# One scatter per pair of expert items on all 128 rows, and the last 2 MB of weights by output column, in a hybrid decoder layer on one core

## Chip, cores and metric

One core of a Trainium2 chip runs the whole program in one launch. The metric is the device time of that core in microseconds (us); lower is better. The engines are TensorE (PE; its weight loads are PEld), VectorE (DVE), ScalarE (ACT), GpSimd (POOL) and SyncE (SP), which here issues nearly all transfers. All data is float32.

## What is computed

A decoder layer on 256 tokens of width 1024: sparse attention and an RWKV-7 mixer behind one input projection, an output projection, cross-attention into 256 memory tokens, and last a mixture of 32 experts, of which each token takes 4. The change lies in the experts, whose reference is, in short:

```python
logits = xt @ router_w + router_b
top_v, top_i = lax.top_k(logits, 4)
gate = jax.nn.softmax(top_v)
# for each expert e, with the tokens tok that chose it and their gates wr:
hb = x[tok] @ mlp1_w[e] + mlp1_b[e]                 # 1024 -> 2048
hg = jnp.minimum(hb[..., ::2], 7.0)
hl = jnp.clip(hb[..., 1::2], -7.0, 7.0)
yb = (hg * sigmoid(1.702 * hg) * (hl + 1)) @ mlp2_w[e] + mlp2_b[e]   # 1024 -> 1024
y[tok] += yb * wr[:, None]
return h + y
```

## The kernel before, in words

An *item* is one expert with up to 64 of its tokens (slots); two items make a pair (`par` 0 is the even, 1 the odd one), so that 128 slots are filled by one gather. In this execution there are 32 items. The weights of one item, 24576 columns of 128 rows (12.58 MB), go through one buffer, `ring`, in six pieces of 2 MB: pieces 0 to 3 hold `mlp1_w`, 4 and 5 hold `mlp2_w`. A piece of the next item is loaded into the place of the same piece as soon as TensorE has used it: SP waits on `piece_used` and issues the load, TensorE waits on `piece_in_c` in `landed` before it reads. Items 6 to 27 are loaded two pieces at a time ("coarse"); for items 10 to 20 1 MB each was loaded earlier into buffers that were free, and POOL copies it into `ring`.

On TensorE an item is written out by hand, in this order: `hidden_bias` (4 products), `hidden` half 0 (pieces 0 and 1, 16 products of 64 slots by 512 columns, two at a time on the two halves of the array's columns), `turn_gates` (two transposes of the gates into PSUM bank 7, which DVE copies to `selgT[par]`), `hidden` half 1 (pieces 2 and 3), `turn_act` of half 0 (two transposes of the activations), `scatter` of the item before (4 products: 64 slots' sums in `yb`, times `selgT`, into four PSUM banks that hold 256 tokens by 1024 columns until the end), `turn_act` of half 1, for an odd item `gather` of the next pair (16 products), and `second` (pieces 4 and 5, 16 products into bank 7). DVE does the clamps and products between them, ACT the sigmoid and the copies of the turned activations and of bank 7 to `yb`. The sums of `yb` hold output columns 0 to 511 in rows 0 to 63 and columns 512 to 1023 in rows 64 to 127 (`o2` is 0 or 1), so each product of `scatter` contracts over 64 rows, and the two of one token tile stand on different rows of the array.

The last item differs: the scatter of the item before stands after piece 0, `turn_act` of half 0 after piece 2, and the end of `mlp2_w` comes in smaller loads (`late_in_0` to `late_in_2`). After it `yb` is copied in two halves of 256 columns, a scatter of 8 products of 256 columns follows, DVE and ACT copy the four PSUM banks out (512 columns each), and SP and ACT issue four stores of 256 KB. The residual `h` is added into the four banks by products with the identity ahead of the last pair (`for bank in range(4)`).

A float32 matmul leaves two records in the trace, so 4 products show as x8.

## Time and profile before

| | |
|---|---|
| runs of the kernel before | 1250.0 us median of 3 (1249.6 to 1250.23) |
| the profiled execution's own time | 1248.68 us |
| its span | 1246.8 us |
| granted TensorE clock, mean | 0.998 |
| weights of 32 items | 32 x 12.58 = 402.7 MB |

The span begins with the first instruction and ends with the last; the execution's own time is 1.9 us longer. The experts' products start at 351.6 us of the span and go on to its end. In a row of the profile, "busy" is the time in which an engine had an instruction at work, "xN" is how many there were, and "idle" with an arrow is what ended a wait. An answer on one DMA issue gives the time from the start of the issuing instruction to the landing of its last byte.

### The profile page before, as it was taken

The numbers are of one execution on the slowest core, as the hardware profiler recorded it, in microseconds if no ns is written. First come the engines' busy times: TensorE is split into PE (matmuls) and PEld (weight loads), VectorE is DVE, ScalarE is ACT, GpSimd is POOL, SyncE is SP. The second block draws the span as 40 slices with busy tenths as digits, with TensorE's granted clock in tenths as the row PEclk, the third lists the DMA queues.
The fourth block names the chain that finished last, engine by engine and source line by source line (L and its number), as shares of the span: only waits on it lengthen the run. The fifth ranks groups of instructions, "written<-read, shape, count | busy, mean of one in ns | idle before, by whom it ended". The sixth has DMA issues, their size and how long they took to land.

```text
span 1246.8 us, 19008 instructions
## 1 busy us (share of the span) xinstructions
PE 1211.5 (97%) x7700; PEld 612.0 (49%) x7700; DVE 373.3 (30%) x855; ACT 191.1 (15%) x435; POOL 76.8 (6%) x118
## 2 busy tenths in 40 slices
PE   9999999999999999999899999999999898989998
PEld 8888778888844343324334343443333232333332
DVE  4457784314064121212122122221212121212111
ACT  2332357214110000000000000000000000000001
POOL 7210012010100000000000001000000000000000
PEclk9999999999999999999999999999999999999999
DMA  7333212394789999999999999999999999999997
GB/s 267 135 137 132 103 37 71 141 427 175 304 340 425 427 428 429 437 429 432 430 433 432 433 430 432 429 432 431 435 423 430 432 433 433 429 429 429 429 427 308
DMA packets 27982, 442.46 MB, mean 355 GB/s; under 512 B 3104, under 2 KB 3232, under 8 KB 5664
## 3 DMA queue, kind: packets, MB, share of 16 engines
q1 hardware_dynamic: 27072, 440.23, 83.9%
q10 hardware_dynamic: 864, 1.57, 0.4%
q8 instruction: 34, 0.56, 0.2%
q14 instruction: 12, 0.10, 0.0%
HBM read 440.75 MB, written 1.05 MB: 354 GB/s over the span
## 4 chain that ended last, share of the span: by engine, by line
PE 75%; DMA 21%; DVE 2%; ACT 1%; issue 1%; SPq 0%; ACTq 0%; POOL 0%; DVEq 0%; POOLq 0%
PE ps L1010 29%; DMA sb_ring<-in_mlp_w 21%; PE ps L1052 11%; PE ps L332 8%; PE ps L986 3%; PE ps L976 3%; PE ps L832 2%; PE ps L783 2%; PE ps L692 2%; PE ps L998 2%; PE ps L1038 1%; PE ps L345 1%; PE ps L567 1%; PE ps L433 1%; PE ps L416 1%
## 5 line engine op out<-in xcount | busy, mean ns | idle before, releaser
L1010 PE MATMUL ps<-sb_ring,sb_xv 128*64 128x512 f32 x2048 | 455.7, 597 | 23.7 <-DMA sb_ring<-in_mlp_w 23.5
L1010 PEld LDWEIGHTS ps<-sb_ring,sb_xv 128*64 128x64 f32 x2048 | 142.1, 137 | 312.0 <-issue 279.6
L1052 PE MATMUL ps<-sb_ring,sb_xv 128*64 128x512 f32 x1024 | 227.0, 595 | 0.3
L1656 DVE TENSOR_SCALAR sb_early<-ps 128x256 f32<-128x256 f32 x64 | 27.2, 425 | 625.1 <-PE ps L1010 619.8
L1052 PEld LDWEIGHTS ps<-sb_ring,sb_xv 128*64 128x64 f32 x1024 | 72.7, 137 | 131.1 <-issue 129.0
L1697 ACT ACTIVATE sb_early<-sb_early 128x256 f32<-128x256 f32 (+2 forms) x69 | 28.2, 408 | 507.1 <-DVE sb_early L1656 500.7
L1697 ACT ACTIVATE sb_early<-ps 128x512 f32<-128x512 f32 (+2 forms) x39 | 21.1, 543 | 274.8 <-PE ps L1052 265.0
L986 PE MATMUL ps<-sb_early 64*128 64x512 f32 x248 | 61.6, 615 | 0.0
L332 PE MATMUL ps<-sb_hnT,sb_wsl 128*128 128x256 f32 x256 | 56.1, 379 | 0.0
L976 PE MATMUL ps<-sb_early,sb_hnT 128*128 128x128 f32 x480 | 56.0, 275 | 0.0
L976 PEld LDWEIGHTS ps<-sb_early,sb_hnT 128*128 128x128 f32 x480 | 54.8, 192 | 0.0
L332 PEld LDWEIGHTS ps<-sb_hnT,sb_wsl 128*128 128x128 f32 x256 | 48.7, 190 | 7.0 <-issue 0.5
L1626 DVE TENSOR_TENSOR sb_xv<-ps,sb_xv 128x512 f32<-128x512 f32 x32 | 22.1, 692 | 54.3 <-PE ps L976 54.0
L1163 DVE SCALAR_TENSOR_TENSOR sb_early<-sb_early 128x256 f32<-128x256 f32 x64 | 37.5, 587 | 2.2
L1038 PEld LDWEIGHTS ps<-sb_ident,sb_xv 128*128 128x128 f32 x128 | 12.9, 141 | 50.9 <-issue 26.0
L998 PE MATMUL ps<-sb_early,sb_hot 32*64 32x512 f32 x256 | 35.9, 613 | 0.0
L692 PE MATMUL ps<-sb_wsl,sb_ox 128*128 128x256 f32 x128 | 31.6, 391 | 0.0
L986 PEld LDWEIGHTS ps<-sb_early 64*128 64x128 f32 x248 | 21.4, 186 | 20.4 <-issue 20.4
L1697 ACT ACTIVATE sb_xv<-ps 128x256 f32<-128x256 f32 x64 | 24.0, 375 | 47.5 <-PE ps L1038 47.5
L1038 PE MATMUL ps<-sb_ident,sb_xv 128*128 128x128 f32 x128 | 28.0, 301 | 0.5 <-DVE sb_xv L1663 0.3
L832 PE MATMUL ps<-sb_hnT,sb_wsl 128*128 128x256 f32 x128 | 28.3, 381 | 0.0
L332 PE MATMUL ps<-sb_ox,sb_wsl 128*128 128x256 f32 x128 | 28.1, 379 | 0.0
(370 smaller groups left out, 1015.5 us busy)
## 6 DMA issues: line engine op xcount, KB each, us to landing
sb_ring<-in_mlp_w SPq DMA_DIRECT2D x55, 4096.0 KB, 19.1
sb_ring<-in_mlp_w SPq DMA_DIRECT2D x54, 2048.0 KB, 17.5
sb_ring<-in_mlp_w SPq DMA_DIRECT2D x11, 3072.0 KB, 15.6
sb_wsl<-in_w_front SPq DMA_DIRECT2D x31, 1024.0 KB, 4.8
sb_ring<-in_mlp_w SPq DMA_DIRECT2D x10, 1024.0 KB, 7.5
sb_wsl<-in_mlp_w SPq DMA_DIRECT2D x3, 1024.0 KB, 8.9
sb_spare<-in_mlp_w SPq DMA_DIRECT2D x2, 1024.0 KB, 9.3
sb_ring<-in_mlp_w SPq DMA_DIRECT2D x4, 512.0 KB, 13.0
```

The costliest lines, as they stand in the source:

```text
L332: mm = pe.matmul(t[:, g * T:(g + 1) * T], w[:, k, g * P:(g + 1) * P], act[:, k, :], start=k == 0, stop=k == KD - 1)
L692: return pe.matmul(t[:, 0:T], memT[:, k, tt * P:(tt + 1) * P], wjob(J_XV[j])[:, k, :], start=k == 0, stop=k == KD - 1)
L832: mm = pe.matmul(t[:, g * T:(g + 1) * T], w[:, k, g * P:(g + 1) * P], hnT[:, k, :], start=k == 0, stop=k == KD - 1)
L976: mm = pe.matmul(psum[:, 4 + k // 4, k % 4 * PAIR:(k % 4 + 1) * PAIR], h[:, tt, k * P:(k + 1) * P], sel[:, tt, :], start=tt == 0, stop=tt ...
L986: mm = pe.matmul(psum[:, 2 * tt + o2, :], selgT[par][r, tt, :], yb[r, :], start=False, stop=False, skip_group_check=True)
L998: return pe.matmul(psum[64 * half:64 * half + 64, 4 + n, :], hot[r, :], bias1[r, :], start=not last, stop=last)
L1010: mm = pe.matmul(psum[64 * half:64 * half + 64, 4 + n, :], xgT[:, k, SLOTS * par:SLOTS * par + SLOTS], ring[:, at + 512 * half:at + 512 * ...
L1038: mm = pe.transpose(psum[:, 6, m * P:(m + 1) * P], actv[:, m * P:(m + 1) * P], ident[:, :])
L1052: mm = pe.matmul(psum[64 * o2:64 * o2 + 64, 7, :], actT[:, 2 * n + m, 64 * q:64 * q + 64], ring[:, at + 512 * o2:at + 512 * o2 + 512], sta ...
L1163: return dve.scalar_tensor_tensor(out=o, in0=x, scalar=s, in1=y, op0=op0, op1=op1)
L1656: dve.tensor_scalar(gl, psum[:, 4 + n, 0:256], 7.0, None, ALU.min).then_inc(sem("glu"), 1)
L1697: return act.activation(o, x, func, **kw)
```

## The change

Sums. `yb` becomes two buffers. An even item's sums go as before to rows 0 to 63 (left columns) and 64 to 127 (right columns) of bank 7; an odd item's go the other way round (`rows(par, o2)`). So `yb[0]` gets the left columns of both items of a pair, one on rows 0 to 63 and one on 64 to 127, and `yb[1]` the right columns. `selgT[o2]` is filled to match, in two copies of 64 rows instead of one of 128. ACT copies bank 7 in two instructions of 64 rows.

Scatter. One scatter per pair of 4 products that contract over all 128 rows. It stands in the even item, after pieces 0 and 1, ahead of `turn_gates`; an odd item has none.

Turns. `turn_act` of half 0 stands in the middle of `hidden` half 1, `turn_act` of half 1 in the middle of piece 4. The gather of the next pair stands between pieces 4 and 5.

Last 2 MB. `mlp2_w`'s second half (piece 5) is laid out by output column: first the columns 0 to 255 of both sides, then 256 to 511. In the loop the product over it reads two blocks of 256 columns, 2048 apart. In the last item the sums of the first 256 columns stay in bank 7 and those of the others go to bank 4; the first are scattered and stored (`last_scatter(0)`) ahead of the wait for `late_in_2`, the others after the last product (`last_scatter(1)`). The residual is added to the left banks by DVE at the end, and only banks 1 and 3 get identity products. There are eight stores of 128 KB instead of four of 256 KB.

```diff
-            def scatter(par):
+            def scatter(cols=slice(0, 512)):
                 for tt in range(TT):
                     for o2 in range(2):
-                        r = slice(64 * o2, 64 * o2 + 64)
-                        mm = pe.matmul(psum[:, 2 * tt + o2, :], selgT[par][r, tt, :], yb[r, :],
+                        mm = pe.matmul(psum[:, 2 * tt + o2, cols], selgT[o2][:, tt, :], yb[o2][:, cols],
                                        start=False, stop=False, skip_group_check=True)
-                mm.then_inc(sem("scattered"), 1)
+                    if cols.stop - cols.start < 512:
+                        mm.then_inc(sem("scattered"), 1)
...
+            def rows(par, o2):
+                return slice(64 * (par ^ o2), 64 * (par ^ o2) + 64)
...
+            closing = view(ring, 20480, 2, 2048)
...
+            def last_scatter(side):
+                pe.wait_ge(sem("y_out"), last_pair * 2 + 3 + side)
+                pe.wait_ge(sem("y_low"), side + 1)
+                if side:
+                    pe.wait_ge(sem("out_left"), 2)
+                    pe.wait_ge(sem("out_right"), 2)
+                scatter(slice(256 * side, 256 * side + 256))
...
                 hidden(i, par, 0, first, last)
+                if not par and not first:
+                    pe.wait_ge(sem("y_out"), i + 1)
+                    scatter()
...
                 if last and par:
-                    second(i, 0, (0,))
-                    turn_act(i, 1)
-                    second(i, 0, (1,), late=("late_in_0",))
-                    second(i, 1, (0,))
-                    second(i, 1, (1,), late=("late_in_1", "late_in_2"))
+                    second_open(i, par, late=True)
+                    pe.wait_ge(sem("act_out"), i * 2 + 3)
+                    landed(i, 5, first)
+                    second_close(i, par, 0, (0, 1)).then_inc(sem("half_used"), 1)
+                    pe.wait_ge(sem("late_in_1"), 16)
+                    second_close(i, par, 1, (0,), bank=4)
+                    last_scatter(0)
+                    pe.wait_ge(sem("late_in_2"), 16)
+                    second_close(i, par, 1, (1,), bank=4).then_inc(sem("piece_used"), 1)
+                    last_scatter(1)
                     return
-                turn_act(i, 0)
...
-                else:
-                    scatter(1 - par)
-                turn_act(i, 1)
+                second_open(i, par, first)
                 if par:
                     pe.wait_ge(sem("selected"), j + 3)
                     gather()
-                for n in range(2):
-                    second(i, n, (0, 1), first)
+                pe.wait_ge(sem("act_out"), i * 2 + 3)
+                landed(i, 5, first)
+                for at in range(0, 2048, 512):
+                    for o2 in range(2):
+                        mm = pe.matmul(view(psum[rows(par, o2), 7, :], 0, 2, 256),
+                                       actT[:, 2 + at // 512 % 2, 64 * (at // 1024):64 * (at // 1024) + 64],
+                                       closing[:, :, at + 256 * o2:at + 256 * o2 + 256],
+                                       start=False, stop=at == 1536, skip_group_check=True)
+                mm.then_inc(sem("piece_used"), 1)
...
-            for bank in range(4):
+            for bank in (1, 3):
...
+                low, high = slice(0, 64), slice(64, 128)
+                dve.tensor_copy(selgT[par][low], view(psum[low, 7, 0:256], 0, TT, P))
+                dve.tensor_copy(selgT[1 - par][high], view(psum[high, 7, 0:256], 0, TT, P)).then_inc(sem("selgT"), 1)
...
+                    dve.tensor_tensor(h[:, tt, cols], psum[:, 2 * tt, cols], h[:, tt, cols], ALU.add) \
+                       .then_inc(sem("out_left"), 1)
...
+                    f(yb[par][0:64, :], psum[0:64, 7, :], ACT.Copy)
+                    f(yb[1 - par][64:128, :], psum[64:128, 7, :], ACT.Copy).then_inc(sem("y_out"), 1)
```

The order on TensorE in an odd item of the loop, from its first piece on. L1010 is `hidden`, L1066 `turn_gates`, L1038 `turn_act`, L986 `scatter`, L976 `gather`, L1052 `second`. Before:

```order
L1010 MATMUL ps<-sb_ring,sb_xv 64x512 x16
L1066 MATMUL ps<-sb_ident,sb_early 128x128 x2
L1010 MATMUL ps<-sb_ring,sb_xv 64x512 x16
L1035 REGISTER_ALU
L1038 MATMUL ps<-sb_ident,sb_xv 128x128 x2
L986 MATMUL ps<-sb_early 128x512 x4
L1035 REGISTER_ALU
L1038 MATMUL ps<-sb_ident,sb_xv 128x128 x2
L1107 REGISTER_ALU
L976 MATMUL ps<-sb_early,sb_hnT 128x128 x16
L1052 MATMUL ps<-sb_ring,sb_xv 64x512 x16
```

The same stretch now, where L1093 is `turn_gates`, L1037 `turn_act`, L1056 piece 4 and L1143 piece 5:

```order
L1010 MATMUL ps<-sb_ring,sb_xv 64x512 x16
L1093 MATMUL ps<-sb_ident,sb_early 128x128 x2
L1010 MATMUL ps<-sb_ring,sb_xv 64x512 x8
L1034 REGISTER_ALU
L1037 MATMUL ps<-sb_ident,sb_xv 128x128 x2
L1010 MATMUL ps<-sb_ring,sb_xv 64x512 x8
L1056 MATMUL ps<-sb_ring,sb_xv 64x512 x4
L1034 REGISTER_ALU
L1037 MATMUL ps<-sb_ident,sb_xv 128x128 x2
L1056 MATMUL ps<-sb_ring,sb_xv 64x512 x4
L1137 REGISTER_ALU
L976 MATMUL ps<-sb_early,sb_hnT 128x128 x16
```

The scatter is gone from the odd item, both turns have moved into weight products, and piece 4 is used ahead of the gather instead of behind it.

The end of the program on TensorE before, from piece 3 of the last item on; L1132 is the last scatter:

```order
L1010 MATMUL ps<-sb_ring,sb_xv 64x512 x8
L1052 MATMUL ps<-sb_ring,sb_xv 64x512 x4
L1035 REGISTER_ALU
L1038 MATMUL ps<-sb_ident,sb_xv 128x128 x2
L1052 MATMUL ps<-sb_ring,sb_xv 64x512 x12
L1132 MATMUL ps<-sb_early 128x256 x8
```

The same end now; L1073 is piece 5 (`second_close`), L985 `scatter`:

```order
L1056 MATMUL ps<-sb_ring,sb_xv 64x256 x8
L1073 MATMUL ps<-sb_ring,sb_xv 64x256 x12
L985 MATMUL ps<-sb_early 128x256
L985 MATMUL ps<-sb_smalls,sb_early 128x256
L985 MATMUL ps<-sb_early 128x256
L985 MATMUL ps<-sb_smalls,sb_early 128x256
L1073 MATMUL ps<-sb_ring,sb_xv 64x256 x4
L985 MATMUL ps<-sb_early 128x256
L985 MATMUL ps<-sb_smalls,sb_early 128x256
L985 MATMUL ps<-sb_early 128x256
L985 MATMUL ps<-sb_smalls,sb_early 128x256
```

The last products over the weights, x4 of 256 columns, now stand between two scatters of four products each, where one scatter of eight products stood behind all of them.

## Rows read from the trace of the kernel before

**Rows 1.** Page: share of the span; 40 slices of DMA busy and GB/s.

```profile
PE 1211.5 (97%) x7700; PEld 612.0 (49%) x7700; DVE 373.3 (30%) x855; ACT 191.1 (15%) x435; POOL 76.8 (6%) x118
DMA  7333212394789999999999999999999999999997
GB/s 267 135 137 132 103 37 71 141 427 175 304 340 425 427 428 429 437 429 432 430 433 432 433 430 432 429 432 431 435 423 430 432 433 433 429 429 429 429 427 308
```

**Rows 2.** Engines' busy time by stretch; last three columns clock, DMA share, GB/s.

```profile
352.00:610.00 258.00, 250.73 (x1234) 91.36 (x1230) 66.24 (x183) 19.16 (x46) 0.41 (x1) 0.99 1.00 424
610.00:936.00 326.00, 323.13 (x1612) 119.60 (x1614) 75.75 (x183) 25.43 (x61) 20.41 (x11) 1.00 1.00 430
936.00:1152.00 216.00, 203.29 (x1014) 77.06 (x1012) 41.44 (x117) 15.67 (x38) 0.00 (x0) 1.00 1.00 431
1152.00:1215.00 63.00, 61.76 (x298) 22.44 (x298) 9.83 (x26) 4.50 (x11) 0.00 (x0) 1.00 1.01 428
```

**Rows 3.** Who waited for whom on PE: total us, times, longest.

```profile
PE ps L1010 <- DMA sb_ring<-in_mlp_w: 23.5, 17, 2.3
```

**Rows 4.** One load of `ring` issued at 402.9 us, and its landing.

```profile
L2191 SPq DMA_DIRECT2D sb_ring<-in_mlp_w x1: 333/333/333, 402.9 to 402.9; - x1
...
DMA to landing us min/median/max: 8.3/8.3/8.3
```

**Rows 5.** Chain that ended last, item 29 from piece 3 on: start, us, what.

```profile
1169.00 3.65 PE ps L1010 x16
1172.65 0.37 PE ps L1038 x2
1173.02 1.92 PE ps L986 x8
1174.94 0.37 PE ps L1038 x2
1175.31 3.57 PE ps L976 x32
1178.88 7.02 PE ps L1052 x32
1185.90 3.63 PE ps L1121 x8
1189.53 1.02 PE ps L998 x8
```

**Rows 6.** Loads of the last item: its piece 3, then its last 0.5 MB.

```profile
L2191 SPq DMA_DIRECT2D sb_ring<-in_mlp_w x1: 333/333/333, 1205.1 to 1205.1; - x1
...
DMA to landing us min/median/max: 23.4/23.4/23.4
...
L2191 SPq DMA_DIRECT2D sb_ring<-in_mlp_w x1: 333/333/333, 1215.8 to 1215.8; - x1
...
DMA to landing us min/median/max: 22.7/22.7/22.7
```

**Rows 7.** The same chain, last item from piece 3 to the last copy.

```profile
1228.90 3.61 PE ps L1010 x16
...
1234.35 0.44 PE ps L1038 x2
1234.79 5.33 PE ps L1052 x24
...
1240.13 0.39 ACT sb_early L1697
...
1240.57 1.19 PE ps L1132 x8
1241.76 0.02 issue
1241.78 0.61 ACT sb_hnT L1697
```

**Rows 8.** Page: DVE reads of 256 PSUM columns. Timeline: last ACT issue. DMA: its landing.

```profile
L1656 DVE TENSOR_SCALAR sb_early<-ps 128x256 f32<-128x256 f32 x64 | 27.2, 425 | 625.1 <-PE ps L1010 619.8
...
1243.52 0.34 ACTq L2029 DMA_DIRECT2D out_h<-sb_hnT  x1
...
out_h<-sb_hnT ACTq DMA_DIRECT2D x1, 256.0 KB, 2.9
```

More of the change, by code:

```diff
@@ L1995, in _, with item @@
             f(gateT, view(psum[:, 6, 0:256], 0, TT, P), ACT.Copy).then_inc(sem("gate_taken"), 1)
-            def item(i, last=False):
+            def item(i, par, last=False):
                 def gate_half(n):
@@ L2007, in item @@
                 gate_half(0)
+                take_turned(0)
+                gate_half(1)
+                take_turned(1)
                 if last:
[L2009 to L2017 removed]
@@ L2019, in _ @@
-            item(0)
-            act.wait_ge(sem("tabled"), 1)
-            last_item = act.value_load(tabi[0:1, 62:63], min_val=NE - 1, max_val=ITEMS)
-            with act.Fori(1, last_item) as i:
-                item(i)
-            item(last_item, last=True)
+                    act.wait_ge(sem("half_used"), 4)
+                    f(yb[0][64:128, 0:256], psum[64:128, 7, 0:256], ACT.Copy).then_inc(sem("y_out"), 1)
+                    for tt in range(TT):
+                        right_half(0, tt)
```

136 lines of the change are left out of this document (75 added, 61 removed).

## The prediction

> **What bounds the kernel now.** I read first the page's shares and its 40 slices [rows 1]. TensorE is busy 97% of the span, which looks like the bound, but the line of DMA says otherwise: from the tenth part of the experts on it is at 9 in every slice, at 423 to 437 GB/s. The table by stretch makes that exact [rows 2]: from 352 to 1215 us the share of busy time of the 16 DMA engines is 1.00 or 1.01 in all four stretches, at 424, 430, 431 and 428 GB/s. An item is 12.58 MB, so at 430 GB/s it takes 29.3 us to load. The work of TensorE on it is shorter. From the chain of an odd item [rows 5]: 32 records of weight products take 7.02 us, and there are three such groups (two of `hidden`, one of `second`); three turns at 0.37; the bias 1.02; the scatter 1.92; the gather 3.57. That is 3 x 7.02 + 3 x 0.37 + 1.02 + 1.92 = 25.1 us for an even item and 28.7 for an odd one, 53.8 for a pair, against 58.5 us of transfer. TensorE makes up the difference by waiting for weights, and the list of waits has it: 23.5 us in 17 waits [rows 3]. It is only that little because in the stretch from 610 to 936 us, where 1 MB of each item is already on the chip, the transfer of a pair is 23.07 MB, 53.6 us, about as long as its products; there TensorE waits for nothing and the DMA share is still 1.00.
>
> So the question for each part of the change is not how much TensorE time it saves, but whether the stream of weights starts earlier, runs without holes, or is followed by less work. The stream's last 0.5 MB was issued at 1215.8 and landed 22.7 us later, at 1238.5 [rows 6]. In the chain, the products over the last 3 MB end at 1234.79 + 5.33 = 1240.1 [rows 7], so transfer and products of the last item run nearly level, and the span ends 6.7 us after the last product.
>
> **The sums' two buffers, `selgT` in two copies, ACT's two copies.** DVE gets one more read of PSUM per item at 0.42 us (a read of 256 columns is 425 ns [rows 8], and half the rows don't make it shorter as far as I can bound it: between 0.2 and 0.42). That is at most 14 us more on an engine that is busy 373 of 1247. The first reader is `second`, which waits on `selgT`; the copies are finished 5 us after `hidden` half 0, and `second` starts 8 us after it. Cover: `hidden` half 1, 7.02 us. ACT copies bank 7 twice at about 0.6 us; the reader now comes one `hidden` half (7 us) later. Both cost nothing; without their cover they would cost 0.4 and 0.6 us per item.
>
> **The scatter.** Before, four products took 1.92 us per item [rows 5], because those of one token tile ran on different rows of the array at the same time: 3.84 us per pair. The new ones stand on all 128 rows, so no two can run together. The nearest row is the residual's: four products of 128 rows by 512 columns with the identity, 3.63 us [rows 5]. I take that value. Per pair the scatter goes from 3.84 to 3.63, a gain of 0.2 us, not the half that "once per pair" suggests. Bounds: 1.92 (as before) and 3.63.
>
> The rule that speaks against this edit is in the Trainium skill, page "TensorEngine Tiling (Array Packing)", section "Performance Considerations": a contraction of 64 rows or fewer gives a factor of two by row tiling, which the change gives up. By it the sum is the same as by the row.
>
> **The turns.** The same number of turns. They now break products on half arrays; in the chain a turn costs 0.37 us wherever it stands, and 2 of its records are worth 0.22 (the gather's 32 take 3.57), so the switch is 0.15 and counted in. `turn_act` of half 1 now waits for DVE, which is ready 1.73 us after `hidden` ends, against 1.76 us of half a piece ahead of it: 0 to 0.15 us per item, as in the last item before. A pair is now 6 x 7.02 + 6 x 0.37 + 2 x 1.02 + 3.63 + 3.57 = 53.6 us, 0.2 less, or as much as before with the waits on DVE. It is under 58.5 either way, and level with 53.6 where 1 MB is on the chip, so the stream sets the pace as before and TensorE only waits elsewhere.
>
> The same page of the Trainium skill says, in "Key Properties", that changing the tiling mode drains the array. By it one more pair of switches per item would cost more than nothing; by the 0.15 us above it is 0.15 us of an item with 2.5 us to spare, and the sum stays.
>
> **When the places in `ring` come free.** Piece 4 of an odd item is used ahead of the gather and without a scatter: 1.92 + 3.57 = 5.5 us earlier. That matters only if the stream ever ran dry. The shortest time to landing that I find once the stream is full is 8.3 us, for piece 4 of item 1, issued at 402.9 us just after that gap [rows 4]; 2 MB take 4.9 us, so 3.4 us of other loads were still ahead of it. Later in the program it is 15 to 25 us. No hole, nothing gained; I keep 0.5 us for it. The first loads of item 1 depend on `hidden` of item 0 alone, which is unchanged. Fewer identity products ahead of the last pair (4 records instead of 8, 1.8 us less) also only make TensorE wait elsewhere. I take the last landing at 1238.5, give or take 0.5.
>
> **The end.** I follow the last item from piece 3, which landed at 1205.1 + 23.4 = 1228.5 [rows 6]. TensorE started on it at 1228.90 [rows 7]; freed of the scatter (1.92) it would be there earlier but must wait for the landing, so it gains only 0.35 us, and everything up to the turn at 1234.35 moves to 1234.0. Then, by the rate of the old chain (24 records of 512 columns in 5.33 us, 1.78 per 1 MB; records of 256 columns taken at half):
> - turn, 0.4: to 1234.4; rest of piece 4, 1.78: to 1236.2 (landed by 1233.6)
> - first 256 columns, 1.78: to 1238.0; half of the others, 0.89: to 1238.9. ACT and DVE meanwhile copy the first sums (0.43)
> - `last_scatter(0)`, half of 3.63, 1.81: to 1240.7
> - last 0.5 MB, 0.89: to 1241.55. Its weights landed at 1238.5, but it stands behind the scatter
> - copies of the sums, 0.43 + 0.06: to 1242.04
> - `last_scatter(1)`, 1.81: to 1243.85
> - DVE's add or ACT's copy of 256 columns, 0.43 + 0.05: to 1244.33, when the last store is issued.
>
> Before, that last issue was at 1243.52 and landed 2.9 us later, with 1 MB of stores under way [rows 8]; the span ended 0.4 us after that. The new last stores are half as large and 0.5 MB. I take 2.5 us, between 1.9 (0.8 to the first byte, 0.6 for the last 256 KB at 410 GB/s, 0.4 to the landing) and 2.9. The span ends at 1244.33 + 2.5 + 0.4 = 1247.2, against 1246.8: **0.4 us later**.
>
> The Trainium skill, page "DMA: Bandwidth & Descriptors", section "Anatomy of one DMA", gives about 2.0 us plus size by 436 GB/s, 2.3 us for 128 KB. By that price the end would be at 1247.0. No row here shows a store of 128 KB.
>
> Where the expected gain goes: behind the last product there is less to do (5.6 us instead of 6.7), but the last product itself is 1.4 us later, because the first half of the scatter, 1.81 us on 128 rows, now stands ahead of it, on a TensorE that the transfers no longer hold up.
>
> **The number.** 1247.2 of span, with the 1.9 us that lay outside it, is 1249.1 for an execution like the profiled one (1248.7). The median of the runs is 1.3 above that, so 1250.4.
>
> **Rivals.**
> 1. *The last scatters are cheap.* If products on 128 rows cost as little as before (0.24 us a record), both last scatters take 0.96 instead of 1.81: the end comes 1.7 us earlier, 1248.7. For it: the old end had 16 records in 2.0 us. Against it: the identity products, 3.63 us for 8 records. The same time results if the stores land in 1.9 us and the last product waits for nothing.
> 2. *The stream runs faster.* If the rate depends on how many loads are queued, the 5.5 us by which piece 4 is freed earlier help where the queue is short: from 352 to 610 us the rate is 424 GB/s against 430 later [rows 2]. All of it made good is 258 x 6/430 = 3.6 us, 1246.8. For it: that row. Against it: the stretch from 1152 to 1215 has the longest queue and 428 GB/s, and the first 15 us of the experts, whose loads the change does not free earlier, hold part of the deficit.
> 3. *Slower: the product over piece 5 reads two blocks.* Its moving operand is now 256 columns and 256 more 8 KB on. No row shows such a read for weights. It decides from the point where TensorE's item passes the transfer's 29.3 us, 2.5 us above 26.8. If the 3.5 us of that piece doubled, an item would be 30.3 and the 30 items from item 2 on would add about 1 us each, more in the 11 items with 1 MB on the chip (3.5 us each): 19 x 1 + 11 x 3.5 = 57 us, 1308. Against it: both blocks are runs of 1 KB, and the products read them no differently from 512 columns in a row. The milder form: the products of 256 columns at the end are bound by their weight loads and take 0.28 us a pair instead of 0.22; 24 pairs are 1.4 us, 1251.8, inside the range.
> 4. *The scatter halves TensorE's work and that shows.* This would need TensorE to be the bound; with DMA at 1.00 in each stretch it isn't, and it is part of case 2's chance.
>
> **How the numbers follow.** The forecast (stream unchanged, end within +1.9 and -0.6 us of mine) gets 0.66; rival 1 0.12; rival 2 with 4 0.12; rival 3 in its strong form or another wait that outlasts the stream's queue 0.10. A measurement of this kernel can tell about 0.2% (2.5 us) from no change. Forecast and rival 1 lie within it: 0.78 the same, 0.12 faster, 0.10 slower. The range takes in the first two cases with their bounds: 1248.7 less 0.6 at the low end, 1250.4 plus 1.9 at the high one, which leaves 0.22 outside; since rival 2 at its weakest ends just below 1248.7, I put the low end at 1247.8 and the high one at 1252.4.
>
> **What would show it.** Right: DMA share 1.00 and 424 to 431 GB/s in the same stretches; waits of TensorE for `ring` at least as long as 23.5 us in all; the scatter x8 at about 3.6 us; last landing near 1238.5; in the chain of the last item a wait for piece 3 near 1228.5, then no wait; last product about 1241.5; last issue of a store about 1244.3. Wrong: a last landing that moved by over 1 us (the stream depends on something else than its own rate), the scatter at 2 us, TensorE without waits in all stretches, or a wait for `late_in_2` in the last item.

## The result: 8 us slower

| | median | range |
|---|---|---|
| before, 6 runs | 1250.12 us | 1249.6 to 1251.19 |
| changed, 5 runs | 1258.01 us | 1256.59 to 1260.6 |

The ratio is 1.0066, with a 95% interval of 1.0055 to 1.0077. That is beyond what I called measurable (0.2%), beyond my range (up to 1252.4), and on the side to which I gave 0.10. A sixth run of the changed kernel had a granted TensorE clock of 0.654 and took 1782 us; it is left out, as no other run was like it. The profiled execution took 1258.88 us, its span is 1256.9, 10.1 longer than before. The changed kernel also scatters more from run to run, 4 us instead of 1.6.

The page of the changed kernel, to be read beside [rows 1]. TensorE is as busy as before and the line of DMA looks as full; only some of its GB/s in the second half of the slices are lower.

```profile
PE 1217.0 (97%) x7600; PEld 609.9 (49%) x7600; DVE 389.4 (31%) x891; ACT 213.2 (17%) x468; POOL 76.6 (6%) x118
DMA  7333302493889999999999999999999999999997
GB/s 268 133 142 123 106 32 70 162 430 146 337 338 427 426 428 432 432 432 432 432 416 432 412 431 410 428 413 402 434 413 434 432 432 433 433 426 428 427 430 289
```

The table by stretch, with the columns of [rows 2], shows where they belong:

```profile
352.00:610.00 258.00, 250.44 (x1200) 89.74 (x1196) 70.09 (x191) 25.42 (x55) 0.00 (x0) 1.00 1.00 424
610.00:936.00 326.00, 317.73 (x1522) 116.23 (x1520) 80.27 (x192) 32.21 (x70) 20.82 (x11) 1.00 0.99 420
936.00:1152.00 216.00, 203.81 (x973) 74.33 (x970) 43.49 (x119) 21.07 (x45) 0.00 (x0) 0.99 1.00 431
1152.00:1215.00 63.00, 62.69 (x295) 22.68 (x295) 11.60 (x30) 5.95 (x13) 0.00 (x0) 1.00 1.01 428
```

Three of four stretches move at the rates of before. From 610 to 936 us it is 420 GB/s instead of 430. 326 us at 10 GB/s less are 3.3 MB, or 7.6 us, most of the 9.3 us by which piece 3 of the last item lands later (1237.85 against 1228.5). Load by load the account closes. In both traces a load of 4 MB lands 9.7 us behind the one ahead of it and one of 3 MB 7.3 us, unless it is late. Summed over the loads issued between 600 and 960 us, what they are late is 0.4 us before and 9.6 us after; the last byte of all weights lands at 1238.5 before and 1247.8 after. This is the stretch in which 1 MB of each item is already on the chip, and in which I had found the products of a pair "level with" its transfer.

TensorE's timeline there, from the end of one odd item to the end of the next (start, us, engine, line, tile, shape, count; in brackets the idle time before and what ended it). L1010 is `hidden`, L985 the scatter, L1056 piece 4, L1143 piece 5, L976 the gather:

```profile
854.23 1.09 PE L998 MATMUL ps<-sb_early,sb_hot 32*64 32x512 f32 x8
855.25 7.09 PE L1010 MATMUL ps<-sb_ring,sb_xv 128*64 128x512 f32 x32
862.27 1.12 PE L985 MATMUL ps<-sb_early 128*128 128x512 f32 x2
...
865.80 0.38 PE L1093 MATMUL ps<-sb_ident,sb_early 128*128 128x128 f32 x2
...
873.55 1.89 PE L1056 MATMUL ps<-sb_ring,sb_xv 128*64 128x512 f32 x8
875.59 0.44 PE L1037 MATMUL ps<-sb_ident,sb_xv 128*128 128x128 f32 x2 [0.15 <-DVE sb_xv L1689]
...
898.09 1.94 PE L1056 MATMUL ps<-sb_ring,sb_xv 128*64 128x512 f32 x8 [0.82 <-DMA sb_ring<-in_mlp_w]
...
902.19 3.84 PE L976 MATMUL ps<-sb_early,sb_hnT 128*128 128x128 f32 x32
...
909.55 1.09 PE L998 MATMUL ps<-sb_early,sb_hot 32*64 32x512 f32 x8
```

The pair takes 909.55 - 854.23 = 55.3 us, where my sum had 53.6 and where before it took 53.76. Two things are to be seen: work that I had too small, and a wait of 0.82 us for weights ahead of piece 4 of the odd item, where before there was none. Four of the pairs in this stretch have that wait, 0.81 to 0.95 us; a pair without it takes 54.5.

Why TensorE waits for weights and the transfers still run below their rate shows in the loads. In the changed kernel the load of pieces 0 and 1 (3 MB, as 1 MB is on the chip) was issued at 862.5 and landed 14.1 us later, at 876.6. The next one, of pieces 2 and 3, could only be issued at 873.9, behind the scatter that now stands between the halves of `hidden`, and landed 14.3 us later, at 888.2:

```profile
L2240 SPq DMA_DIRECT2D sb_ring<-in_mlp_w x1: 332/332/332, 862.5 to 862.5; - x1
DMA to landing us min/median/max: 14.1/14.1/14.1
...
L2240 SPq DMA_DIRECT2D sb_ring<-in_mlp_w x1: 333/333/333, 873.9 to 873.9; - x1
...
DMA to landing us min/median/max: 14.3/14.3/14.3
```

So at 873.9 only 2.7 us of earlier loads were left. That is the last byte of the slowest of the 16 DMA engines; others had nothing left, as the share of busy time around it shows (0.52, then 0.91, at 221 and 270 GB/s). The load landed 11.6 us behind the one ahead of it, 1.9 us late:

```profile
870.00:872.00 2.00, 2.00 (x12) 0.78 (x12) 0.00 (x0) 0.38 (x1) 0.00 (x0) 1.00 1.03 442
872.00:874.00 2.00, 2.00 (x13) 0.60 (x10) 0.14 (x1) 0.00 (x0) 0.00 (x0) 1.00 0.52 221
874.00:876.00 2.00, 1.85 (x12) 0.51 (x8) 1.93 (x7) 0.42 (x1) 0.00 (x0) 1.00 0.91 270
```

In the kernel before, the load of the same pieces was issued at 863.0, when the one ahead (issued at 855.6, landing 14.0 us later) had 6.6 us to go, and it landed at 879.3, 9.7 us behind it:

```profile
L2191 SPq DMA_DIRECT2D sb_ring<-in_mlp_w x1: 333/333/333, 855.6 to 855.6; - x1
...
DMA to landing us min/median/max: 14.0/14.0/14.0
...
L2191 SPq DMA_DIRECT2D sb_ring<-in_mlp_w x1: 332/332/332, 863.0 to 863.0; - x1
...
DMA to landing us min/median/max: 16.3/16.3/16.3
```

Below I call this time, from the issue of a load to the landing of the load ahead of it, the *margin*. I took it for each load between 620 and 935 us; its smallest value is 4.8 us before and 1.8 us after. In the changed kernel four loads of this kind, issued at 707.8, 763.1, 818.5 and 873.9 with margins of 1.8 to 3.0 us, land 2.9, 1.9, 1.7 and 1.9 us late, 8.4 of the 9.6 us.

The margin also shows that the kernel before was close to its limit. The six loads of a pair here, two of 3 MB and four of 4 MB, take 53.5 us, the products 53.76. TensorE frees the places 0.3 us later in each pair than the transfers would need them, and the queue of loads makes it up: the load of pieces 4 and 5 that an odd item sets free has margins of 6.2, 5.9, 5.6, 5.3, 5.0 and 4.8 us in the six pairs. The queue had a few us to give at the start of the stretch, and six pairs nearly used them up.

### The profile page after: what moved, and what is told of

Same layout as the page of the kernel before. It is cut to its first block, busy times and chain, and to the rows that moved or that the text cites. A ratio compares the mean times of both kernels' runs of the same rounds, so it can differ in the third digit from the quotient of the medians.

```text
span 1256.9 us, 18844 instructions
## 1 busy us (share of the span) xinstructions
PE 1217.0 (97%) x7600; PEld 609.9 (49%) x7600; DVE 389.4 (31%) x891; ACT 213.2 (17%) x468; POOL 76.6 (6%) x118
## 4 chain that ended last, share of the span: by engine, by line
PE 77%; DMA 18%; DVE 3%; issue 1%; ACT 1%; DVEq 0%; SPq 0%; POOL 0%; ACTq 0%; POOLq 0%
PE ps L1010 23%; DMA sb_ring<-in_mlp_w 18%; PE ps L1143 8%; PE ps L332 8%; PE ps L1056 7%; PE ps L976 4%; PE ps L985 4%; PE ps L692 2%; PE ps L832 2%; PE ps L783 2%; PE ps L998 2%; PE ps L1037 2%; PE ps L567 1%; PE ps L345 1%; DVE sb_early L1189 1%
## 5 line engine op out<-in xcount | busy, mean ns | idle before, releaser
L1010 PE MATMUL ps<-sb_ring,sb_xv 128*64 128x512 f32 x2048 | 460.7, 597 | 9.1 <-DMA sb_ring<-in_mlp_w 8.9
L1010 PEld LDWEIGHTS ps<-sb_ring,sb_xv 128*64 128x64 f32 x2048 | 138.9, 137 | 282.9 <-issue 267.5
L1056 PE MATMUL ps<-sb_ring,sb_xv 128*64 128x512 f32 (+1 forms) x528 | 124.7, 594 | 17.6 <-DMA sb_ring<-in_mlp_w 17.6
L1143 PE MATMUL ps<-sb_ring,sb_xv 128*64 128x512 f32 x496 | 112.5, 595 | 0.0
L1056 PEld LDWEIGHTS ps<-sb_ring,sb_xv 128*64 128x64 f32 x528 | 35.3, 137 | 80.8 <-issue 79.9
L1143 PEld LDWEIGHTS ps<-sb_ring,sb_xv 128*64 128x64 f32 x496 | 34.3, 137 | 64.0 <-issue 62.2
L976 PEld LDWEIGHTS ps<-sb_early,sb_hnT 128*128 128x128 f32 x480 | 54.7, 192 | 12.2 <-issue 12.2
L976 PE MATMUL ps<-sb_early,sb_hnT 128*128 128x128 f32 x480 | 57.6, 278 | 0.0
L332 PE MATMUL ps<-sb_hnT,sb_wsl 128*128 128x256 f32 x256 | 56.1, 379 | 0.0
L1733 ACT ACTIVATE sb_smalls<-ps 64x512 f32<-64x512 f32 (+1 forms) x32 | 18.7, 585 | 142.3 <-PE ps L1143 132.7
L1037 PEld LDWEIGHTS ps<-sb_ident,sb_xv 128*128 128x128 f32 x128 | 12.9, 141 | 56.5 <-issue 34.8
L985 PE MATMUL ps<-sb_early 128*128 128x512 f32 (+1 forms) x68 | 34.8, 593 | 0.6 <-ACT sb_early L1733 0.6
L1733 ACT ACTIVATE sb_early<-ps 64x512 f32<-64x512 f32 (+3 forms) x38 | 20.6, 542 | 83.3 <-PE ps L1143 78.8
L985 PE MATMUL ps<-sb_smalls,sb_early 128*128 128x512 f32 (+1 forms) x68 | 33.0, 567 | 0.0
```

The source lines that it names most:

```text
L332: mm = pe.matmul(t[:, g * T:(g + 1) * T], w[:, k, g * P:(g + 1) * P], act[:, k, :], start=k == 0, stop=k == KD - 1)
L976: mm = pe.matmul(psum[:, 4 + k // 4, k % 4 * PAIR:(k % 4 + 1) * PAIR], h[:, tt, k * P:(k + 1) * P], sel[:, tt, :], start=tt == 0, stop=tt ...
L985: mm = pe.matmul(psum[:, 2 * tt + o2, cols], selgT[o2][:, tt, :], yb[o2][:, cols], start=False, stop=False, skip_group_check=True)
L1010: mm = pe.matmul(psum[64 * half:64 * half + 64, 4 + n, :], xgT[:, k, SLOTS * par:SLOTS * par + SLOTS], ring[:, at + 512 * half:at + 512 * ...
L1037: mm = pe.transpose(psum[:, 6, m * P:(m + 1) * P], actv[:, m * P:(m + 1) * P], ident[:, :])
L1056: mm = pe.matmul(psum[rows(par, o2), bank, cols], actT[:, m, 64 * q:64 * q + 64], ring[:, at + 512 * o2 + cols.start:at + 512 * o2 + cols. ...
```

## Experiments

My theory after the result (A): in this stretch the queue of loads gets short, for TensorE's work of a pair is as long as the transfer and the places in `ring` come free late and two pieces at a time; what the change adds (0.7 us of work a pair, a scatter ahead of the release of pieces 2 and 3, an earlier need of piece 4) empties it. The rivals are that the work alone counts (B), that the transfers are slower because of the new reads or the new order wherever they stand (C, G), that the gather's place is to blame (D) or the 128-row scatter (E), and that the stream covers 1 us of added work everywhere (F). Letters further on belong to one run alone and are explained in its expectation.

### Changed kernel with loads of 2 MB (e1)

```diff
             with sp.Fori(COARSE, AHEAD_AT) as i:
-                coarse_item(i, i)
+                item(i, i)
...
                 piece(i, 0, at=(0, AHEAD.start))
-                coarse_item(i, i, 2)
+                item(i, i, range(2, PIECES))
```

> The changed kernel with every load of the ring 2 MB (one piece) instead of 4 MB for items 6 to 27. In the trace of the changed kernel a pair of items takes 55.4 us between 688 and 910 us of the span, against 53.8 before; 54.5 of it is TensorE's own work and 0.8 to 0.95 a wait ahead of piece 4 of the odd item, where one 4 MB load of pieces 4 and 5 must have landed. Theory A (two parts: work that grew by 0.7 us a pair, and a wait of 0.9 that comes from the 4 MB load being needed ahead of the gather): the wait goes, the work stays, 1258.4 - 5 = 1253 to 1255. Rival B (the work alone sets the time, the wait is a symptom): 1257 to 1259. Rival C (the transfers themselves run slower because of the new reads): 1257 to 1259, with a DMA share of 1.00 at under 425 GB/s.

Measured 1253.63 us, ratio to before 1.0032 (1.0021 to 1.0044). The wait in this stretch is gone and the margin is never under 8.8 us. TensorE's pair is then its own work alone, from gather to gather 54.50 us:

```profile
731.67 3.84 PE L976 MATMUL ps<-sb_early,sb_hnT 128*128 128x128 f32 x32
786.17 3.84 PE L976 MATMUL ps<-sb_early,sb_hnT 128*128 128x128 f32 x32
```

```profile
352.00:610.00 258.00, 252.89 (x1209) 90.52 (x1210) 72.87 (x197) 25.84 (x56) 1.89 (x1) 1.00 1.00 421
610.00:936.00 326.00, 322.12 (x1548) 117.69 (x1546) 77.92 (x189) 32.97 (x71) 18.93 (x10) 1.00 1.01 429
936.00:1152.00 216.00, 205.39 (x982) 74.96 (x978) 45.30 (x124) 20.69 (x45) 0.00 (x0) 1.00 1.01 429
```

The number fits theory A, the reason for it only in part. The DMA share is 1.01 in the middle stretch: with 54.5 us of work a pair the stream has no holes. The margins say why. With smaller loads, each issued as soon as its own piece is free, the smallest margin of a pair is 11.8 us at the start of the stretch and falls by 0.7 in each, the work of 54.5 less a transfer of 53.8, so that 8.8 us are left at its lowest. What keeps this kernel at 1253.6 is that loads of 2 MB run a little slower than those of 4 MB: 421, 429 and 429 GB/s against 424, 430 and 431 before. Over 258, 326 and 216 us that is 1.8 + 0.8 + 1.0 = 3.6 us, and the rest is the end. From landing to landing the same shows: a load of 2 MB takes 4.89 us, so two take 9.78, where one of 4 MB takes 9.71; over the 55 loads that were split this is 3.9 us, and the last byte lands 4.4 us later than before. I had put the remaining loss down to the work; e11, below, shows that it isn't.

### Changed kernel with half a scatter in the loop (e2)

```diff
-                for tt in range(TT):
+                for tt in range(TT if cols.stop - cols.start < 512 else 1):
```

> The changed kernel, in which the scatter of each pair but the last leaves out the second token tile (2 products instead of 4), so the sums of tokens 128 to 255 are incomplete. It takes 1.8 us of TensorE work out of each even item and lets pieces 2 and 3 come free 1.8 us earlier. Theory A: work of a pair 54.5 - 1.8 = 52.7, under the 53.6 of its transfer; the stream is full again between 610 and 936 us (430 GB/s), total 1250 to 1251.5. Rival B: the same, 1250 to 1251.5. Rival C (slower transfers for another reason than a short queue, such as the reads of piece 5 in two blocks): 1257 to 1259.

Measured 1249.25 us, ratio 1.0000 (0.9990 to 1.0010). The pair takes 53.46 us, with a wait of 0.68 for weights in it, so the transfer sets the pace again; 431 GB/s between 610 and 936 us, smallest margin 4.5 us. The loop's scatter leaves out half of the tokens here, so this kernel measures time and nothing else. The reads of piece 5 in two blocks, the two buffers of sums and ScalarE's and VectorE's extra copies are all still there, so rival C falls.

### Kernel before, gather between pieces 4 and 5 (e3)

```diff
+                second(i, 0, (0, 1), first)
                 if par:
                     pe.wait_ge(sem("selected"), j + 3)
                     gather()
-                for n in range(2):
-                    second(i, n, (0, 1), first)
+                second(i, 1, (0, 1), first)
```

> The kernel before with one edit: the gather of the next pair stands between pieces 4 and 5 instead of ahead of piece 4. TensorE's work is the same; in the trace of before the 4 MB load of pieces 4 and 5 lands 4.4 us before an odd item reads it (landing at 782.2, read from 786.6), and the edit takes 3.7 of that. Theory A: 0.7 us left, no wait or one of under 0.3 us a pair, 1250 to 1252. Rival D (the gather's place by itself is what costs): 1254 to 1258.

Measured 1252.16 us, ratio 1.0016 (1.0006 to 1.0025): slower, 0.2 us above the range of theory A and 1.8 below that of rival D, and not by the wait that I had reckoned with; TensorE doesn't wait for weights in these pairs. What I had missed is that the same instructions take longer there. The gather is 3.84 instead of 3.74 us and there are two more changes between 64-column and 128-column products; the pair goes from 53.76 to 54.11 us:

```profile
735.27 3.84 PE L976 MATMUL ps<-sb_early,sb_hnT 128*128 128x128 f32 x32
789.38 3.84 PE L976 MATMUL ps<-sb_early,sb_hnT 128*128 128x128 f32 x32
```

A third of a microsecond, six times, is 2 us. How the 0.35 us divide between the gather and the changes of shape I didn't separate. The stretch has 427 GB/s and a smallest margin of 3.5.

### Kernel before with the order of the changed one (e4)

```diff
                     if 1024 * (k + 1) % PIECE == 0:
...
+                        if k == 3 and n:
...
+                            turn_act(i, 0)
...
                 hidden(i, par, 0, first, last)
+                if not first and not (last and par):
+                    pe.wait_ge(sem("y_out"), i + 1)
+                    scatter(1 - par)
...
+                second(i, 0, (0,), first)
                 turn_act(i, 1)
+                second(i, 0, (1,), first)
                 if par:
...
                     gather()
-                for n in range(2):
-                    second(i, n, (0, 1), first)
+                second(i, 1, (0, 1), first)
```

> The kernel before with the order of the changed one and the scatters of before: a scatter of 64 rows (1.92 us) in each item between the halves of the hidden product, both turns inside weight products, the gather between pieces 4 and 5. One buffer of sums, the old layout of the last 2 MB and the old end. Theory A: work of a pair about 54.3 us (as in the changed kernel, since the scatters cost 3.84 against 3.54 to 3.63 and the waits for VectorE inside piece 4 are the same), pieces 2 and 3 free 1.9 us later in both items, piece 4 needed 5.6 us earlier: nearly the whole loss, 1254 to 1258. Rival E (the 128-row scatter and the two buffers cause the loss): 1250 to 1251.

Measured 1256.5 us, ratio 1.0056 (1.0040 to 1.0073). The pair takes 54.85 us, the stretch has 421 GB/s and a smallest margin of 3.4. The order alone, with scatters of 64 rows, one buffer of sums, the old layout and the old end, brings most of the loss, 7.0 of about 8 us. Rival E falls: without the 128-row scatter the loss is nearly all there.

```profile
610.00:936.00 326.00, 322.53 (x1588) 116.31 (x1586) 74.75 (x180) 26.38 (x60) 20.86 (x11) 1.00 1.00 421
```

### Kernel before with 0.9 us of idle work a pair (e5)

```diff
-                for tt in range(TT):
+                for tt in list(range(TT)) * 3:
                     mm = pe.transpose(psum[:, 7, tt * P:(tt + 1) * P], selg[:, tt, :], ident[:, :])
```

> The kernel before, in which turn_gates does its two transposes three times over, with the same result; nothing else is moved. It adds 8 short records, about 0.9 us, to TensorE's work of a pair of items. Theory A (between 610 and 936 us of the span the work of a pair, 53.8 us, is already as long as its transfer, so each 0.1 us added shows about six times over; elsewhere transfers cover it): pair 54.6 us there, total +5, 1254 to 1256. Rival F (the stream of weights covers 1 us of work everywhere, as its DMA share of 1.00 suggests): 1249.5 to 1250.5.

Measured 1253.92 us, ratio 1.0030 (1.0021 to 1.0039). The pair is 54.64 us, 0.88 more, and six times that is 5.3; measured were 4.2. The stretch has 424 GB/s, a smallest margin of 2.1. No order was changed here: work alone, put where the kernel had seemed to have it for nothing, costs nearly its full length, and rival F falls. TensorE doesn't wait for weights in these pairs either. It is the slower of the two, and the small margin follows from that: at the load of pieces 4 and 5 it goes 3.3, 2.9, 2.2, 2.1 and 2.1 us from the second pair on, until the stream idles as long in each pair as TensorE is longer.

```profile
734.48 3.74 PE L976 MATMUL ps<-sb_early,sb_hnT 128*128 128x128 f32 x32
789.12 3.74 PE L976 MATMUL ps<-sb_early,sb_hnT 128*128 128x128 f32 x32
```

### Both kernels without the 11 MB loaded ahead (e6, e7)

GpSimd's copies of these 11 MB into `ring` go as well.

```diff
-                sp.dma_start(aheads[n], a["mlp_w"][AHEAD_AT + n, :, AHEAD]).then_inc(sem("ahead_in"), 16)
...
-                piece(i, 0, at=(0, AHEAD.start))
-                coarse_item(i, i, 2)
+                coarse_item(i, i)
```

> The kernel before without the 11 MB that are loaded ahead of the experts: all of each item's weights go through the ring in the loop, and GpSimd copies nothing. It adds 11.5 MB to the stream, 26.8 us at 430 GB/s. All theories: 1275 to 1278. It is there to be compared with the changed kernel without them, next.

> The changed kernel without the 11 MB loaded ahead. A pair then takes 58.5 us of transfer in every stage, against 54.5 of TensorE work. Theory A: the loss in the loop is gone, what is left is the end, 0 to 1.2 us over the kernel before without them: 1275.5 to 1279. Rival G (the changed order or the reads of piece 5 cost wherever they stand): 8 us over it, 1283 to 1286.

Measured 1275.05 us for the kernel before and 1275.86 for the changed one, 0.8 apart, with four runs each that spread over 2 us. Where every pair has 58.5 us of transfer, the whole loss in the loop is gone: 432 GB/s from 610 to 936 us in both. The last byte of the weights lands at 1263.8 and 1263.1 us, not later in the changed kernel. The changed order and the reads in two blocks cost nothing there; rival G falls. What remains is the end.

### The 11 MB spread over twice as many items (e9, e10)

```diff
-                sp.dma_start(aheads[n], a["mlp_w"][AHEAD_AT + n, :, AHEAD]).then_inc(sem("ahead_in"), 16)
+                sp.dma_start(aheads[n], a["mlp_w"][AHEAD_AT + 2 * n, :, AHEAD]).then_inc(sem("ahead_in"), 16)
...
+            with sp.Fori(AHEAD_AT // 2, AHEAD_AT // 2 + len(aheads)) as j:
+                i = j * 2
...
+                coarse_item(i, i, 2)
+                coarse_item(i + 1, i + 1)
```

`AHEAD_AT` is 6 instead of 10.

> The changed kernel with the 11 MB loaded ahead spread differently: 1 MB for each even item from 6 to 26 instead of 1 MB for each of the items 10 to 20. The bytes in the ring's stream are the same; a pair now has 24.1 MB, 56.0 us, of transfer over 22 items, instead of 23.1 MB, 53.6 us, over 11. TensorE's work of a pair, 54.5 us, fits under 56.0. Theory A: the loss in the loop goes without touching the order or the scatter, 1249.5 to 1251.5. Rival B2 (the wait ahead of piece 4 stays, since it comes from the 4 MB load being needed 5.5 us earlier, whatever slack there is): 1252 to 1256.

> The kernel before with the same spreading. Its work of a pair, 53.8 us, was 0.1 over the transfer of 11 of the items. Theory A: little to gain, 1248.5 to 1250. It is the comparison for the changed kernel with the same spreading.

Measured 1249.18 us for the changed kernel (ratio to before 1.0000, 0.9991 to 1.0009) and 1248.91 for the one before (0.9996, 0.9987 to 1.0006). All of the 8 us are back, with the changed order, scatter and end untouched. The stretch in the changed kernel:

```profile
610.00:936.00 326.00, 316.81 (x1520) 115.77 (x1520) 74.49 (x190) 31.82 (x69) 10.31 (x6) 1.00 1.00 431
```

Its pair takes 55.9 us, of which 1.4 is a wait for weights; its smallest margin is 5.2 us, and the last byte of the weights lands at 1238.5 us, as before. Rival B2 (the 4 MB load alone makes the wait, whatever the slack) falls.

### Changed kernel, loads of 2 MB, one turn later (e11)

This is e1 with one more edit, in odd items:

```diff
                     if q:
-                        turn_act(i, 1)
+                        if late or not par:
+                            turn_act(i, 1)
...
                 if par:
+                    turn_act(i, 1)
                     pe.wait_ge(sem("selected"), j + 3)
```

> The changed kernel with loads of 2 MB (as in e1_after_fine) and, in odd items, the turn of the second half behind piece 4 instead of in its middle, so that TensorE doesn't wait there for VectorE. In e1 a pair took 54.50 us with no wait for weights, 1253.6 in all. Theory A (the pair's own work sets the time there): 0.3 us less a pair, 54.2, and 1.5 to 2 us less in all, 1251.5 to 1252.5. Rival I (the 0.7 us came from elsewhere, such as the reads in two blocks): 1253.6 as before.

A miss. Measured 1253.63 us, the same as e1. The work did shrink, and by more than I thought, from 54.50 to 53.92 us a pair (the gather is back at 3.74):

```profile
784.42 3.74 PE L976 MATMUL ps<-sb_early,sb_hnT 128*128 128x128 f32 x32
...
838.34 3.74 PE L976 MATMUL ps<-sb_early,sb_hnT 128*128 128x128 f32 x32
```

But it bought nothing, since with loads of 2 MB the stream had no holes to be filled (margins of 8.8 us and more in e1, 11.4 in this one). Rival I had the number right, 1253.6, but not its reason: the 0.6 us did come from the turn and the gather. So the work of a pair doesn't count by itself. What it has over the transfer is first taken from the queue of loads. With 4 MB at a time that queue is short, 4.8 us at its least even in the kernel before, and once it is used up each further us of a pair is lost, as in e5. With 2 MB it lasts through the stretch.

### Kernel before with the new end, and the best version (e8, e12)

The end of the changed kernel, with scatters of 64 rows and one buffer of sums, in the kernel before:

```diff
+                    second_open(i, late=True)
...
+                    second_close(i, 0, (0, 1)).then_inc(sem("half_used"), 1)
+                    pe.wait_ge(sem("late_in_1"), 16)
+                    second_close(i, 1, (0,), bank=4)
+                    last_scatter(0)
+                    pe.wait_ge(sem("late_in_2"), 16)
+                    second_close(i, 1, (1,), bank=4).then_inc(sem("piece_used"), 1)
+                    last_scatter(1)
```

> The kernel before with the end of the changed one and its own scatters: the last 2 MB laid out by output column, the first 256 columns scattered and stored ahead of the last product, eight stores of 128 KB, the residual of the left banks added by VectorE; the scatters are those of 64 rows (about 1.0 us each in the end instead of 1.9), with one buffer of sums, and the loop keeps the order of before. Theory A: the last product ends 0.7 us later than before, the last stores leave 1.1 us sooner relative to it and are smaller, in all 0.7 to 1.0 us less than before: 1249.0. Rival H (the new end costs by its many small steps whatever the scatters take): 1250 to 1251.

Measured 1249.13 us against 1249.73, ratio 0.9996 (0.9987 to 1.0005). It is the number of theory A (1249.0), not that of rival H (1250 to 1251), but the 0.6 us are within the noise: inconclusive. Its chain shows ScalarE in the way: two stores of the first columns are issued ahead of its copy of the last sums.

```profile
1240.89 0.37 ACTq L2061
...
1241.71 0.34 ACTq L2061
...
1242.17 0.39 ACT sb_early L1725
```

The last version is e8 with the 11 MB spread as in e10 and these two stores moved to SyncE:

```diff
+                    if not side:
+                        sp.wait_ge(sem("out_right"), tt + 1)
+                        sp.dma_start(out[0, tt * P:(tt + 1) * P, 512:768], h[:, tt, 512:768]).then_inc(sem("out_done"), 16)
```

> The kernel before with three edits: the spreading above, the new end with scatters of 64 rows (as in e8), and in that end the stores of the first 256 columns all issued by SyncE, because in e8 ScalarE issued two of them (0.37 us each) ahead of its copy of the last sums, which began at 1242.17 although the last product was done about 1 us earlier. Theory A: 1 us less than e8 by the copy, 0 to 0.5 by the spreading: 1247.5 to 1248.5. Rival J (the end is set by the landing of the stores, not by what is ahead of them): 1249.

Measured 1246.91 us (1246.51 to 1248.58, 11 runs) against 1249.51 for the kernel before, ratio 0.9980 (0.9971 to 0.9989): faster than both, by 2.6 and by about 11 us, and more than expected (1247.5 to 1248.5). Rival J, by which the landing of the stores sets the end at 1249, falls. The chain of its end:

```profile
1235.52 2.59 PE ps L1071 x24
1238.11 1.06 PE ps L986 x8
1239.17 1.04 PE ps L1071 x8
...
1240.24 0.39 ACT sb_early L1725
...
1240.67 0.73 PE ps L986 x4
```

The first scatter costs 1.06 us on 64 rows, and the copy follows the last product at once. How the 2.6 us divide among the three edits I didn't separate; e10 alone was 0.6 and e8 alone 0.6, neither beyond its noise.

### The experiments side by side

GB/s are those between 610 and 936 us; the margin is that of the 33 to 36 loads of 4 or 3 MB issued between 620 and 935 us (59 and 60 of 3 and 2 MB in e1 and e11), each worked out as the landing of the load ahead less the issue. "Late" is the sum, over the loads issued between 600 and 960 us, of what each lands later behind the one ahead than 9.71 us for 4 MB, 7.30 for 3 MB or 4.89 for 2 MB.

| kernel | pair, us | smallest margin, us | late, us | GB/s | median, us |
|---|---|---|---|---|---|
| before | 53.8 | 4.8 | 0.4 | 430 | 1249.5 to 1250.1 |
| e2, half scatter | 53.5 | 4.5 | 0.1 | 431 | 1249.3 |
| e3, gather moved | 54.1 | 3.5 | 3.5 | 427 | 1252.2 |
| e5, extra work | 54.6 | 2.1 | 4.6 | 424 | 1253.9 |
| e4, new order | 54.9 | 3.4 | 6.4 | 421 | 1256.5 |
| changed | 55.3 | 1.8 | 9.6 | 420 | 1258.0 |
| e9, changed, spread | 55.9 | 5.2 | 0.1 | 431 | 1249.2 |
| e1, changed, 2 MB | 54.5 | 8.8 | 0.3 | 429 | 1253.6 |
| e11, and turn later | 53.9 | 11.4 | 0.2 | 429 | 1253.6 |

With 4 MB loads, the rate is whole where the margin stays over 4.4 us and falls where it goes to 3.5 or less; the median rises with what the loads are late. The smallest margin doesn't order the losses by itself (e5 has less of it than e4 and loses less). The two rows of 2 MB loads stand apart: full queue, lower rate.

## Why the prediction was wrong

**The view that misled.** I read a DMA share of 1.00 at some 430 GB/s from 352 to 1215 us as a stream that sets the pace everywhere, with room. In the second stretch it was full by a hair, and only because a queue of 6 us lasted just long enough. I had both figures, 53.8 us of work and 53.6 of transfer a pair, and wrote that they were level; from that follows that this stretch has no cover at all, and that whatever is added to a pair there counts some six times. Instead I wrote that "the stream sets the pace as before and TensorE only waits elsewhere". That is the step that failed: in the changed kernel a pair takes TensorE 54.5 us, 55.3 with its wait, against 53.5 of transfer, and in four pairs the stream loses about 2 us each (8.4 in all). e5 shows the same with an edit that is nothing but work.

**The work of a pair, 53.6 us.** Measured 54.5 (e1). The term was mis-sized by 0.9. The scatter was as forecast or a little better: 865.80 - 862.27 = 3.5 us for its 8 records, against 3.63 by the row of the identity products. The waits for VectorE inside piece 4, which I gave 0 to 0.15 us an item, are 0.29 wherever no wait for weights stands ahead of piece 4: from the start of piece 4's first half to the turn it is 2.04 us (873.55 to 875.59), of which 1.75 is work. The remainder are changes of shape: the gather takes 3.84 where it stands now and 3.74 where it stood. I had charged a turn at 0.37 wherever it stands, and the gather nothing for its new neighbours. The Trainium skill, "TensorEngine Tiling (Array Packing)", section "Key Properties", says that a change of tiling mode drains the array; I cited it and dismissed it as 0.15 us "of an item with 2.5 us to spare". The trace agrees in so far as the same products took 0.35 us a pair longer with two more such changes (e3), in a stretch in which nothing was to spare; that it is the drain which took them is not shown.

**"No hole, nothing gained."** I looked for the shortest time to landing, found 8.3 us at 402.9, and took the 15 to 25 us of later loads for a long queue (the shortest in this stretch is 14.0). Most of those 15 us are the load's own transfer, 7 or 10 us for 3 or 4 MB. The margin, the figure that matters, was 5 to 10 us there. I also looked only at what the change frees earlier (piece 4) and not at what it frees later: pieces 2 and 3 of an even item, 11.4 us behind pieces 0 and 1 (873.9 - 862.5) instead of 7.4 (863.0 - 855.6). The diff and the order show that plainly.

**The need of piece 4.** I counted only its release. It is also read ahead of the gather and without a scatter, 5.5 us earlier, and as the load is one of 4 MB, all of pieces 4 and 5 must have landed. That is the wait of 0.8 to 0.95 us in four odd items of the stretch. It had no term in my sum.

**The end.** This part held in mechanism and nearly in size. From the landing of piece 3 to the end of the span I had 18.7 us (before 18.3); measured were 1256.9 - 1237.85 = 19.05. The chain of the changed kernel:

```profile
1237.89 3.68 PE ps L1010 x16
...
1243.42 0.44 PE ps L1037 x2
1243.85 1.88 PE ps L1056 x16
1245.73 2.59 PE ps L1073 x24
1248.32 1.92 PE ps L985 x8
1250.24 1.04 PE ps L1073 x8
...
1251.31 0.39 ACT sb_early L1733
...
1251.82 1.98 PE ps L985 x8
```

The wait is for piece 3 as said, and the first scatter, 1.92 us (I had 1.81), stands ahead of the last product, which waits for no transfer. The second is 1.98, the last product 1.04 instead of 0.89. The last stores landed faster than the 2.5 us I took:

```profile
out_h<-sb_hnT ACTq DMA_DIRECT2D x1, 128.0 KB, 2.0
out_h<-sb_hnT SPq DMA_DIRECT2D x1, 128.0 KB, 2.2
```

The Trainium skill, "DMA: Bandwidth & Descriptors", section "Anatomy of one DMA", gives a fit by which this size takes 2.3 us, but for transfers issued by GpSimd; these stores, issued by ScalarE and SyncE, took 2.0 to 2.2, nearer to it than my value. From the last byte of the weights to the end of the span it is 8.4 us before and 9.1 after, 8.4 in e10 and 9.0 in e9, so the new end costs 0.6 to 0.7 us in these traces, against my 0.4. The medians put it at 0.8 (e6 and e7) and 0.3 (e9 and e10), neither clear of the noise. So of the 10.1 us between the two traced spans 9.3 are the stream's and 0.7 the end's; the medians lie only 7.9 apart.

**The signs.** The scatter (3.5 us), the waits of TensorE for `ring` (26.5 us in all), the wait for piece 3 and the free last product came as I had listed them for a right prediction. Of those for a wrong one, one came: the last landing moved by over 1 us, by 9.3.

**The rivals.** I had one on the slow side, and its mechanism, a slow read in two blocks, does not occur: e2, e7 and e9 have that read and lose nothing in the loop. Its reckoning held the very point that the forecast missed: it let a loss begin when an item passed 29.3 us, but charged the 11 items with 1 MB on the chip the full 3.5 us, as items without cover. I didn't ask what that meant for the smaller terms of the forecast. "Another wait that outlasts the stream's queue" shared its 0.10 and was not worked out, although it is what happened.

## What to carry to other kernels

A stream at full rate is no proof of slack: compare work and transfer for each stage by itself, and where they are level, price every added instruction at its full length times the number of rounds, less what the queue of loads holds when the stage begins. When an edit moves instructions in a loop that refills one buffer, list for each load when its place comes free and when its data is needed, earlier and later both, and compare with the landing of the load ahead, not with its own time to landing. If such a stage turns out tight, it may be cheaper to move bytes than instructions: here spreading 11 MB over twice as many items gave back all that the new order cost.

## What the runs showed of the hardware

- The 16 DMA engines don't finish together. At the end of before, their mean share was 0.99 from 1234.0 to 1235.4 us, 0.51 in the next us and 0.14 from there to 1238.5, when the last byte landed. In the changed kernel, with 2.7 us of queue left by the landing of the slowest engine, the share over all was already 0.52 for 2 us.
- How long the queue must be by the last landing is known only roughly. Of the loads issued between 610 and 936 us in all fourteen traces, 25 of the 35 with a margin under 4.2 us landed over 0.25 us late, by up to 2.9. Of the 507 with a longer one 3 did, by up to 0.7. One load in the changed kernel had 2.8 us and was on time, so the margin is not all that decides.
- Two loads of 2 MB took 9.78 us from landing to landing and one of 4 MB 9.71. Over the kernel that was about 4 us (e1).
- A gather of 32 records took 3.74 us behind a turn, and 3.84 us right behind products over 64 slots (e3, e1, e11).
- Four products over 128 rows by 512 columns took 3.5 us, four over 64 rows, two at a time on different rows of the array, 1.92 us.
